# TensorE waits for its own work at five places of the feed-forward stages

## What is computed

```python
def _swiglu(x, w1, w2):
    gt, up = jnp.split(x @ w1, 2, axis=-1)
    return (jax.nn.silu(gt) * up) @ w2

def second_block(x, rel_bias, ...):
    for l in range(DEPTH):
        x = _layer_norm(DN_ALPHA * x + 0.5 * _swiglu(x, ffn1_w1[l], ffn1_w2[l]), ln1_g[l], ln1_b[l])
        mix = _token_mix(x, w_in[l], ..., rel_bias, ...)
        x = _layer_norm(DN_ALPHA * x + mix, ln2_g[l], ln2_b[l])
        x = _layer_norm(DN_ALPHA * x + 0.5 * _swiglu(x, ffn2_w1[l], ffn2_w2[l]), ln3_g[l], ln3_b[l])
    return x
```

## Time and profile before

| | us |
|---|---|
| median of 3 runs | 2404.16 |
| the runs | 2394.35, 2404.16, 2404.68 |
| span of the profiled execution, first to last instruction | 2401.1 |
| TensorE busy in it | 2316.8 |
| VectorE busy | 1499.2 |
| ScalarE busy | 1190.5 |
| GpSimd busy | 243.2 |

### The profile page before, as it was taken

One profiled execution on the slowest core, in us unless ns is written; L12 is line 12 of the kernel. 1 busy time (PEld: TensorE's weight loads), 2 busy tenths in 40 slices (PEclk: granted clock), 3 DMA queues, 4 the chain that ended last, 5 costly groups with the idle time before them and its releaser, 6 DMA issues. The chain is left out here.

```text
span 2401.1 us, 45036 instructions
## 1 busy us (share of the span) xinstructions
PE 2316.8 (96%) x17296; PEld 2095.1 (87%) x17296; DVE 1499.2 (62%) x2663; ACT 1190.5 (50%) x1934; POOL 243.2 (10%) x272
## 2 busy tenths in 40 slices
PE   6999999999999999999999899999999998999998
PEld 4777677788779699999988899999999987999998
DVE  5487984453578865665487666654655677667554
ACT  6344743643345646434376554543543565555433
POOL 0012000000013000022010100221121101000220
PEclk8999999999999999999999999999999999999999
DMA  7321034343243044555553335455455453344552
GB/s 288 120 87 45 2 110 166 145 174 141 70 133 120 1 170 179 175 197 184 185 202 139 124 126 191 158 181 187 157 183 187 160 185 137 140 161 157 185 185 86
DMA packets 61844, 355.61 MB, mean 148 GB/s; under 512 B 6208, under 2 KB 19712, under 8 KB 20352
## 3 DMA queue, kind: packets, MB, share of 16 engines
q1 hardware_dynamic: 61552, 353.55, 41.2%
q10 hardware_dynamic: 144, 0.01, 0.0%
HBM read 349.29 MB, written 1.10 MB: 146 GB/s over the span
## 5 line engine op out<-in xcount | busy, mean ns | idle before, releaser
L244 DVE TENSOR_TENSOR w_lo<-ring,w_hi 128x1024 fp32r<-128x1024 f32 x638 | 812.9, 1307 | 453.4 <-ACT w_hi L230 452.9
L286 PE MATMUL psum<-x_hi,w_hi 128*128 128x256 f32 (+1 forms) x3376 | 1028.2, 305 | 12.4 <-DVE x_lo L583 3.2
L288 PE MATMUL psum<-x_hi,w_lo 128*128 128x256 f32 (+1 forms) x3376 | 1010.5, 299 | 0.0
L287 PE MATMUL psum<-x_lo,w_hi 128*128 128x256 f32 (+1 forms) x3376 | 1008.3, 299 | 0.0
L230 ACT ACTIVATE w_hi<-ring 128x1024 fp32r<-128x1024 f32 (+1 forms) x638 | 643.8, 1049 | 313.3 <-PE psum L288 144.7
L286 PEld LDWEIGHTS psum<-x_hi,w_hi 128*128 128x128 f32 x3376 | 634.8, 188 | 48.2 <-issue 11.4
L287 PEld LDWEIGHTS psum<-x_lo,w_hi 128*128 128x128 f32 x3376 | 635.7, 188 | 25.6 <-issue 1.7
L288 PEld LDWEIGHTS psum<-x_hi,w_lo 128*128 128x128 f32 x3376 | 635.3, 188 | 23.4
L1875 PE MATMUL psum<-h_hi,w_lo 128*128 (+1 forms) x640 | 180.1, 281 | 0.0
L1872 PE MATMUL psum<-h_hi,w_hi 128*128 (+1 forms) x640 | 180.0, 281 | 0.0
L1874 PE MATMUL psum<-h_lo,w_hi 128*128 (+1 forms) x640 | 180.0, 281 | 0.0
(11 more groups left out here) (332 smaller groups left out, 2861.0 us busy)
## 6 DMA issues: line engine op xcount, KB each, us to landing
ring<-wstream SPq DMA_DIRECT2D x320, 1024.0 KB, 4.8
x<-xT SPq DMA_DIRECT2D x2, 1024.0 KB, 8.2
x<-ctxT SPq DMA_DIRECT2D x2, 1024.0 KB, 10.7
rel_bias<-bias_by_distance SPq DMA_DIRECT2D x2, 1024.0 KB, 7.7
fox_bias<-forgetting_sums SPq DMA_DIRECT2D x2, 1024.0 KB, 7.5
cst<-consts SPq DMA_DIRECT2D x1, 1534.0 KB, 10.6
wk<-wk_once SPq DMA_DIRECT2D x8, 128.0 KB, 4.3
kk_sw<-kk_sw SPq DMA_DIRECT2D x8, 128.0 KB, 5.8
```

Source lines behind the costliest of these rows:

```text
L244: dve.tensor_tensor(w_lo[:, c % 2, h], ring[:, (c + 2 * i) % RING, h], w_hi[:, c % 2, h].bitcast(F32), ALU.subtract).then_inc(split_done.s ...
L286: pe.matmul(o, w_hi[:, c, w_cols], hi, start=first, stop=False)
L287: pe.matmul(o, w_hi[:, c, w_cols], lo, start=False, stop=False)
L288: return pe.matmul(o, w_lo[:, c, w_cols], hi, start=False, stop=last)
```

## The change

Two waits are added on TensorE. After `pe_side_by_side`, in the three feed-forward stages that follow a norm, it waits until the last matmul of that chunk has ended. After each part of the bias products it waits until the last of them has ended. Nothing is removed or moved.

```diff
@@ RelBias.pe
                         pe.wait_ge(mixed.sem, self.m0 + k - 5)
                     mm = pe.matmul(self.bank(k), const("flip"), rel_bias[:, 2 * k:2 * k + 2, :], start=True, stop=True)
                 mm.then_inc(parted.sem, 1)
+                pe.wait_ge(parted.sem, self.f0 + part + 1)
@@ ffn_stage, up_chunk
                             if norm and first(i, s):
                                 pe_side_by_side(pe, hi, lo, lambda k: norm.before(pe, k))
+                                pe.wait_ge(chunk_done.sem, g0[0] + 1)
                             else:
                                 pe_columns(pe, i, s, hi, lo, S)
                         pairs_of(pe, up_chunk, bias and bias.pe)
```

## The result

| | before | after |
|---|---|---|
| median, us (20 runs each, same chip) | 2399.78 | 2404.22 |
| lowest and highest | 2394.35, 2404.68 | 2398.76, 2408.46 |
| span of the profiled execution | 2401.1 | 2399.1 |
| TensorE busy in it | 2316.8 | 2311.3 |

The ratio of after to before is 1.0017, with a 95% interval of 1.0010 to 1.0024: by it 4.1 us more (2.4 to 5.8); the two medians are 4.4 apart. The change makes the kernel a little slower. The profiled execution of after is 2.0 us *shorter* than that of before, so one pair of executions says the opposite of forty runs. Why that can be is half of what follows.

A forecast was written before the change was run, and what follows sets the result against it. The prediction took TensorE (96% busy) to bound the kernel. From 2404.2 us, waits +1.9 and the bias stage -6.7 gave 2399.4 us; the range for 8 in 10 was 2377 to 2409.

The forecast's parts named there:

- the price of the waits: At the five added TensorE waits: 0.38 us each, 1.9 us in all, bounds 0.8 to 4.2 us.
- two rates: TensorE's matmul stream runs at 113.3 or 117.8 ns a matmul, with the same lines, shape and full clock.
- a rate that lasts: In the feed-forward stages a rate, once there, stays until the next disturbance and doesn't change within a stage.
- the prediction's own sign: A feed-forward stage changing rate in its middle, or an untouched stage changing, would show the rate isn't set by the start.
- the 6.9 us of 1536 matmuls: Saving in one normed stage if all 32 chunks behind its side-by-side chunk run fast; 20.7 us in three stages.
- the nearest row taken as the rule for a restart: Restarts follow the nearest profiled start: fast behind the bias (1012.75), slow in the normed stages (918.41, 1510.85).
- the term of -6.7 us: Bias stage: fast rate behind the products saves 6.3 us behind part 1 and 0.4 us behind part 0.
- the slow rate as a property of the stages: All four feed-forward stages run at 117.8 ns, up and down; only two chunks ahead of the bias products run fast.
- rival 3: At the five waits no rate changes and only the waits cost: 2406.1 us (2405.0 to 2408.4), chance 0.23.
- rival 1: Every restart is fast, in the bias stage and the three normed stages: 2378.7 us, chance 0.30.
- Rival 4: TensorE loses its queue's lead, so 126 later chunk borders cost some 0.22 us each: +27.7 us, 2433.8 us, chance 0.04.
- Rivals 1 and 2: The second of these: the three normed stages go fast, the bias stage doesn't; 2385.4 us, chance 0.12.

The follow-up runs named there:

- the held sequencer: Against the changed kernel, an empty instruction is added on TensorE behind each of the five waits; 2404.01 us, ratio 1.0025 (1.0011 to 1.0038).
- a run 10 us shorter than the others: Not a numbered run: one of the runs before the change, nothing changed, 10 us shorter than the others; its own time isn't given.
- The five drains: Against the changed kernel, a drain of TensorE's pipeline stands in the place of each of the five waits; 2396.01 us, ratio 1.0001 (0.9988 to 1.0014).

## Why the prediction was wrong

**Right: the bound and the price of the waits.** TensorE was the bound, nothing hid the waits, 1.9 us was forecast and 1.9 measured. That the sums agree so well is luck in part: the single price was a little less than 0.38 at four places (0.32), and more at one (0.61, and up to 0.71 in other traces with this wait), within the bounds of 0.16 to 0.84. The Trainium skill, "TensorE: Matmul & The Clock Gate" (Single matmul latency; LDWEIGHTS), gave an estimate of 0.27 for each (the 109 ns in it are that page's gap for 256 columns, see the end of this section); the rows show 0.32 where nothing stands between wait and load.

**Right: two rates. Right in part: a rate that lasts.** The counts named for a slow and a fast stage (970 and 1008; 818 and 850) are what the traces of later kernels show, 970 and 1007 or 1008, 817 and 849. One sentence was wrong: "within a stage it doesn't change". Every stage that was fast up to its last up chunk turned slow where the down chunks begin; with the normed waits alone two stages turned fast there. By the prediction's own sign (a stage that changes its rate in its middle) the step on which the sums of the rivals rest, that the rate is set by a start, is wrong too. So no stage gave the 6.9 us of 1536 matmuls; the most that was seen is 4.7. Down chunks from 2325 to 2375 us in that kernel, 443 against the 427 of a slow stretch:

```profile
2325.00:2375.00 50.00, 50.00 (x443) 1.00 0.38 134
```

**Wrong: the nearest row taken as the rule for a restart.** This is the step that failed: the term of -6.7 us. In its place the runs showed nothing, +0.7 us (-2.6 to +4.1) for the bias waits alone, with 817 matmuls in 96 us where 850 were named. The forecast let the bias stage go fast because the start at 1012.75 was fast: same stage, same operands. That start is itself not fixed: of the seven traces of the kernel before the two chunks behind it are fast in two, and they are slow in the second trace of after and in that of the held sequencer. A row of one execution was taken for a property of a place. The rows against it, 918.41, 1481.37 and 1510.85, were counted as three starts of another kind; the one at 918.41 varies from execution to execution as well, and of the four one was fast in that trace. In the changed kernel it was 1 of 15 in three traces.

**Wrong: the slow rate as a property of the stages.** "All four feed-forward stages run at the slow one" was true of the one execution that was there to read. In three of seven the last normed stage is fast. So rival 3, the case that came closest, was short as well: it priced the waits alone, +1.9, against +4.1 measured. All the cases priced a restart as something that leaves the rate or betters it. A restart where the stream may already be fast can also end that, and in seven of nine stages with a start there it did: some 2.0 us more, worked out from three of seven traces, that no case had. The remark under rival 1, that a run 10 us shorter than the others could be a change of rate, was on the track: such executions exist, and the change ends some of them.

**The other rivals.** Rival 4, the lost lead, is out: after shows no gap at later borders, and its counts are those of the earlier trace rows. Rivals 1 and 2 wanted fast normed stages behind the wait; in three traces of the changed kernel none of nine is.

**The base.** 2404.16 was the middle of three runs spread over 10 us. Twenty runs of the same kernel gave 2399.78. A forecast in absolute time carried that error of 4.4 us, more than the effect. That 2404.22 lies within 2377 to 2409, and hardly off the 2404.2 that the sum began with, is luck: from the true base the change was to give 2395.0.

**What stays open.** Against what the moment of a start is measured. 113.33 ns are 272 periods of 2.4 GHz. Slow steps are uneven, 116 to 120 ns in the normed stages of the first trace of before, but over the chunks 4 to 21 of such a stage three steps, one hi and lo group, take 353.33 ns, 848.0 periods, against 816 at the fast rate. Slow is thus 32 periods more for three matmuls; that fits a second beat to which the slow stream is bound, but no run here shows one. The Trainium skill, the same page (Back-to-back issue gap), gives 109 ns for 256 columns as the gap of isolated matmuls, and for a stream of weight loads and matmuls some 81 ns at 128 columns and 131 at 512, with nothing for 256 and no second rate. No long stretch of 128x256 read here has 109.

No version was found that beats both kernels: a start costs 0.3 to 0.8 us, a fast stage is worth 4.7 as far as was seen, but no start was found that is fast reliably. The five drains come out even with before, 1.0001 (0.9988 to 1.0014).

## What to carry to other kernels

Before a rate, a gap or a wait is read off one trace, look whether the same place has it in a second execution of the same program; a stretch that nobody edited serves as the control. A wait put in to reset an engine can change its state either way: price what it may lose where the state is already good, not only what it may win. And compare the spread of the runs with their median: here the missing short runs showed where the rest of the loss was.

## What the runs showed of the hardware

- A stream of matmuls 128x256, each with its own weight load, runs at 113.3 or 117.8 ns a matmul at the full granted clock (816 or 848 periods of 2.4 GHz for three). Which it is varies in many places between executions of one program; it lasts over more than 1000 matmuls.
- The rate can change without idle time where the code goes over to another loop: at 80 borders from up to down chunks all ten stages that came at 113.3 ns went on at 117.8, and 7 of the 70 that came at 117.8 went on at 113.3.
- With starts at regular moments the choice is nearly regular: every fourth chunk in one kernel, chunks 8 and 14 in another whose starts differ by a few nanoseconds, alike in three stages.
- A TensorE wait for its own last matmul costs 0.32 us where the weight load stands right behind it, and 0.61 to 0.71 at the entry of a loop, where register instructions stand between the two.
- A second and a third empty instruction behind a TensorE wait did not delay the next start by more than some 4 ns each time; the first one delayed it by some 0.1 to 0.2 us.
